# Recurrence scores: four level planes multiplied by masks, four copied over them under masks, two adds for a strided sum

## The reference

```python
def hgrn_chunk(S, q, k, v, logf):
    b = jnp.cumsum(logf, axis=1)
    o_inter = jnp.einsum('bchk,bhkv->bchv', q * jnp.exp(b), S)
    decay = jnp.exp(jnp.where(causal, b[:, :, None] - b[:, None, :], -jnp.inf))
    scores = jnp.sum(q[:, :, None] * k[:, None, :] * decay, axis=-1)
    o_intra = jnp.einsum('btsh,bshv->bthv', scores, v)
    k_dec = k * jnp.exp(b_last[:, None] - b)
    S_new = jnp.exp(b_last)[..., None] * S + jnp.einsum('bchk,bchv->bhkv', k_dec, v)
```

## Time and profile before

| | us |
|---|---|
| median of 3 runs | 1724.35 (1719.77 to 1724.97) |
| the profiled execution | 1728.1 |
| its span | 1726.3 |
| TensorE busy, of the span | 1547.2 (90%) |
| VectorE busy, of the span | 707.1 (41%) |
| ScalarE busy, of the span | 461.9 (27%) |
| L784, 36 of them | 41.5 |
| L786, 36 of them | 64.6 |

### The profile page before, as it was taken

The page is one execution under the profiler, slowest core; times in us unless marked ns, Lnnn a source line. Parts: engine busy times, 40 slices in busy tenths (PEclk is TensorE's granted clock), DMA queues, the critical chain, the costliest instruction groups (busy, mean ns, idle before and its releaser), DMA issues. The chain is left out here.

```text
span 1726.3 us, 22053 instructions
## 1 busy us (share of the span) xinstructions
PE 1547.2 (90%) x7497; PEld 1056.2 (61%) x7498; DVE 707.1 (41%) x1465; ACT 461.9 (27%) x1040; POOL 235.8 (14%) x417
## 2 busy tenths in 40 slices
PE   5999999986899898989789999999799929999996
PEld 3566565665465565655568888888678724444442
DVE  4368886886244453444432222233332241222121
ACT  2233343332233343334332222122232200111110
POOL 1000111011222222222100000000000001122221
PEclk8999999987799998989889999999999959999998
DMA  7001200000402001000055667233343392987973
GB/s 243 26 0 59 78 1 26 1 27 1 143 1 63 1 30 35 1 27 1 27 168 183 199 198 251 80 110 110 132 118 110 110 316 76 336 240 227 302 206 49
DMA packets 119369, 186.03 MB, mean 108 GB/s; under 512 B 9507, under 2 KB 82262, under 8 KB 117222
## 3 DMA queue, kind: packets, MB, share of 16 engines
q1 hardware_dynamic: 107750, 134.41, 24.4%
q0 software_dynamic: 11520, 50.34, 10.0%
HBM read 154.38 MB, written 30.34 MB: 107 GB/s over the span
## 5 line engine op out<-in xcount | busy, mean ns | idle before, releaser
L972 PE MATMUL psum<-attention_part,kept 128*128 128x384 f32 (+1 forms) x576 | 205.6, 513 | 0.7 <-DVE attention_part L1205 0.7
L2166 PE MATMUL psum<-moe_part,kept 128*128 x384 | 172.3, 602 | 6.4 <-issue 4.9
L972 PEld LDWEIGHTS psum<-attention_part,kept 128*128 128x128 f32 (+1 forms) x576 | 110.2, 196 | 78.7 <-issue 20.9
L1438 PE MATMUL psum<-split 128*128 128x368 f32 x384 | 140.6, 366 | 2.5 <-DVE split L1584 2.5
L498 PE MATMUL psum<-kept,recurrence_part 128*128 128x368 f32 x384 | 124.7, 480 | 10.0 <-PEq L236 5.0
L1427 PE MATMUL psum<-kept,sample_part 128*128 128x368 f32 x384 | 131.8, 487 | 1.3 <-PEq L873 1.3
L1440 PE MATMUL psum<-split 128*128 128x368 f32 x384 | 127.3, 332 | 0.0
L2166 PEld LDWEIGHTS psum<-moe_part,kept 128*128 128x128 f32 x384 | 72.3, 193 | 89.6 <-issue 89.6
L1439 PE MATMUL psum<-split 128*128 128x368 f32 x384 | 127.0, 331 | 0.0
L503 PE MATMUL psum<-recurrence_part,kept 128*128 128x512 f32 (+1 forms) x288 | 125.9, 593 | 0.0
L1593 DVE TENSOR_TENSOR merge_part<-merge_part,psum 128x368 f32<-128x368 f32 x48 | 25.8, 538 | 220.2 <-ACT merge_part L1527 220.2
(11 more groups left out here) (312 smaller groups left out, 2527.3 us busy)
## 6 DMA issues: line engine op xcount, KB each, us to landing
sample_part<-merge_gates POOLq DMA_DIRECT2D x16, 1024.0 KB
merge_part<-cache_kT SPq DMA_DIRECT2D x64, 256.0 KB, 3.4
merge_part<-cache_v SPq DMA_DIRECT2D x64, 256.0 KB, 3.1
moe_part<-w_gate SPq DMA_DIRECT2D x16, 1024.0 KB, 6.2
moe_part<-w_up SPq DMA_DIRECT2D x16, 1024.0 KB, 12.6
moe_part<-w_down SPq DMA_DIRECT2D x16, 1024.0 KB, 14.0
recurrence_part<-w_in SPq DMA_DIRECT2D x8, 1024.0 KB, 9.2
sample_part<-merge_out POOLq DMA_DIRECT2D x16, 512.0 KB, 6.4
```

Source lines behind the costliest of these rows:

```text
L972: mm = pe.matmul(bank_of(("z", h, i))[:ROWS[i], 0:384], K["xT"][:, k, cols(i)], Wb[h % 2][:, k, :], start=(k == 0), stop=(k == KC - 1))
L1438: pe.matmul(bank_of(u, 2 * j + 1), wh[w % 2][:, k, ch], xh[b][:, k, :], start=(k == 0), stop=False)
L2166: mm = pe.matmul(psum[:, 2 + par, :], XT[par][:, k, :], K["GU"][:, bass.ds(KC * b + k, 1), :], start=(k == 0), stop=(k == KC - 1))
```

## The change

The buffer `AM` holds four planes in place of eight. The first four planes are multiplied by their masks into it, which sets to 0 every element whose pair belongs to none of them. The other planes (four, or one in tile 0) are copied over it with a predicated copy, element by element where their mask isn't zero; the mask's floats are read as integers for that. As a pair belongs to one plane at most, nothing that is needed is overwritten. Then two adds bring four planes to two and two to one, the second into `AT`. A drain stands between each two. Two instructions of VectorE (L784, L786) become four (L784, L786, L788, L790 in the changed kernel); the lines behind them move down by four, so L806 becomes L810. Nothing changes on the other engines or in the order of the rest.

```diff
@@ -420,7 +420,7 @@
-        AM, AT, kdT = sb(8 * P), sb(2, P), sb(2, P)
+        AM, AT, kdT = sb(4, P), sb(2, P), sb(2, P)
@@ -774,16 +774,20 @@
                 lev = psum[:, 2 + 2 * (s % 2):4 + 2 * (s % 2), :].rearrange("p a (b c) -> p (a b) c", c=P)
-                am = AM[:r, 0:nl * r].rearrange("p (l c) -> p l c", l=nl)
+                mask = (lmask0 if i == 0 else lmask)[:r, :, :r]
                 dve.wait_ge(leveled, s + 1)
                 if s == 0:
                     dve.wait_ge(c_in, 48)
                 if s >= 2:
                     dve.wait_ge(o_done, s - 1)
                 dve.drain()
-                dve.tensor_tensor(am, lev[:r, 0:nl, :r], (lmask0 if i == 0 else lmask)[:r, :, :r], ALU.mult)
+                dve.tensor_tensor(AM[:r, :, :r], lev[:r, 0:4, :r], mask[:, 0:4, :], ALU.mult)
                 dve.drain()
-                dve.tensor_reduce(AT[:r, s % 2, :r], am.rearrange("p l c -> p c l"), AX_X, ALU.add).then_inc(at_done, 1)
+                dve.copy_predicated(AM[:r, 0:nl - 4, :r], mask[:, 4:nl, :].bitcast(I32), lev[:r, 4:nl, :r])
+                dve.drain()
+                dve.tensor_tensor(AM[:r, 0:2, :r], AM[:r, 0:2, :r], AM[:r, 2:4, :r], ALU.add)
+                dve.drain()
+                dve.tensor_tensor(AT[:r, s % 2, :r], AM[:r, 0, :r], AM[:r, 1, :r], ALU.add).then_inc(at_done, 1)
```

## The result

The changed kernel took 1709.12 us in the median of five runs (1704.79 to 1715.82), beside 1724.35 us (1719.73 to 1726.35) for the kernel before: a ratio of 0.9928 with an interval of 0.9899 to 0.9957, 12 us faster. In a second, longer comparison (12 executions against 35) the ratio was 0.9934 (0.9911 to 0.9957), 11.4 us. The forecast was 9.7 us and 1714.6, with a range from 1709 to 1723: the first median lies at its lower edge. The profiled execution has a span of 1714.0 us against 1726.3.

What follows compares the result with a forecast made beforehand. TensorE was taken to bound the recurrence to 343 us, then a ring of VectorE and TensorE. 2.5 + 5.4 + 1.8 (clock) = 9.7 us, taken from 1724.35, gave 1714.6 us; range 1709 to 1723.

Steps and rivals of the forecast that it cites:

- The bound: Recurrence: TensorE sets the pace to 343 us, VectorE is busier behind; VectorE saves 28 us, most beside other work.
- The price of a tile: Four new VectorE instructions hold a full tile for 2.21 us against 3.08, 0.87 us less.
- rival 1: Copy under a mask takes two passes (1721 us) or the strided reduce's rate (1719 us); chance 0.20.
- rival 3: Copy under a mask far from streaming, so tiles get longer: 7.7 us slower, 1732 us; chance 0.07.
- 95 to 343 us: TensorE is full; only three of its four waits for L687 shrink, by 0.87, 0.87 and 0.74: 2.5 us.
- the wait before step 8: TensorE's fourth wait for L687, 1.34 us before 175.30, was to keep its length.
- 343 to 431 us: Last tiles of the recurrence: five give 0.87 us each, tiles 30 and 34 0.5 each: 5.4 us.
- the wait for the root: VectorE's new state waits for GpSimd's L674; in tiles 25, 28 and 31 this swallows the whole saving.
- The clock: End of recurrence: shorter waits put one group of scores at the high TensorE clock, some 1.8 us.
- The sign that was named: TensorE's mean clock over the last 80 us should be above 0.81.
- the ring: Last nine tiles: L784, L786, L806 on VectorE, L518, L519 on TensorE, next L784; the change shortens one link.

Runs made afterwards that it cites:

- the copy-twice kernel: The changed kernel with the copy under masks made twice, a drain between: 1725.06 us, ratio 1.0006 to the kernel before.
- the filler: The changed kernel with four needless products more in each of steps 30 to 35, before TensorE's wait for the new state: 1712.57 us, ratio 0.9915 to the kernel before.

## Why the prediction was right, and where it wasn't

**The bound.** Right. VectorE was to be spared 28 us; by the time that the tiles hold it, it was spared 25.6 (32 x 0.80; its busy time fell by 31.3, from 707.1 to 675.8), and some 9 arrived. Doubling the copy took just this gain back.

**The price of a tile.** Right within a tenth: 2.28 us against 2.21 forecast. The product came out at 693 ns (0.69 forecast), the adds at 427 and 294. The step that no row showed, the copy under a mask, takes 734 ns; taking the row of the same number of streams for it was right, two passes or the reduce's rate (rival 1) wrong, and so was rival 3. The prediction says that what goes is above all the stride of the reduce. The runs show the number of elements first: with half the planes and the stride kept, 0.58 of the 0.80 us were there already. The Trainium skill's advice on the page "VectorE: DVE Perf Modes", section "Rules for kernel authors", sets the number of operations against the number of semaphores, not against their form as the prediction has it; the trace does not follow it, since four instructions of 512, 512, 256 and 128 elements in a row hold VectorE for 2.28 us and two of 1024, one with a stride, for 3.08. The copy-twice kernel holds it as long with five.

**95 to 343 us.** Forecast: 2.5 us, with the wait before step 8 left as it is. The wait for L687 fell by 2.2 us; the waits before 249 and 342 us vanished, that before 316 shrank from 1.28 to 0.44, and that of step 8 stayed (1.34 to 1.70). From the first L519 to that of step 26 the two kernels took 249.3 us (in both traces) and 245.7 and 245.5, so 3.7 us were gained here. A wait of 0.7 us for ScalarE's L584, in both traces before and in neither after, accounts for part of what the sum had left out.

**343 to 431 us.** The wait of L518 fell to 17.4, not to 16 as forecast. From step 26's L519 to the last L556 it was 81.9 and 82.3 us before and 75.8 and 77.7 after: 5.3 us in the mean, with a scatter of 1.9, where 5.4 were forecast without the clock. That the savings of the tiles 25, 28 and 31 end in the wait for the root fits VectorE's waits for it (19.3 us over 95 to 440 us, 9.6 before); that these tiles give their share once ScalarE's order is changed is not shown, as the clock moved as well. Forecast without the clock, the recurrence was to lose 7.9 us; the pairs of traces give 9.7 and 8.4.

**The clock.** This term, 1.8 us, is the step that failed: the runs show nothing in its place. I read from the earlier trace rows that a wait of 2 us or less leaves the clock high, and counted 1.8 us for one group that would be high. In the first trace of the changed kernel the last group ran at the low level (3.23 us) behind a wait of 1.99 us, and in the second trace all four were low. The L518 groups of the steps 30, 33, 34 and 35 add up to 11.67 and 12.27 us in the two traces before, and to 10.87 and 12.75 in the two of the changed kernel: no difference. One trace with few groups at each level does not give a rule: with ScalarE's order changed, groups behind waits of 2.94 and 3.24 us were at the high level. The sign that was named, a mean clock above 0.81, came (0.83), but says nothing: the kernel before had 0.86 in its second trace. The clock is worth 6 us there, as the filler showed, but the change does not collect them. Without this term the forecast is 7.9 us and lies 1.1 us under the mean of the two pairs (9.0); with it, it is 0.7 above.

**The size in all.** The sum came out near for a reason that is partly luck: the clock's 1.8 us, which did not come, made up for 1.2 us before step 26 that were not counted. The timed gains were 15.2 us between the first medians and 11.4 us with more executions (interval 7.4 to 15.3). The second agrees with the recurrence's 9, and its median, 1714.22 us, with the forecast of 1714.6; the first median was 5.5 us under the forecast, within what the attention stage scatters by (14 us over the twelve traces). That nothing behind the recurrence gained is shown by two pairs of traces to no better than this scatter.

## What to carry to other kernels

A sum over planes with a stride is paid for by every element, and laying the data out otherwise only moves the stride to the writer: have fewer elements instead (here masks that exclude each other let one plane be copied over another), and fold what is left by adds of contiguous halves. Before you count a saving on an engine, follow the ring it stands in: here the ring took in about 9 of 26 us, and one split wait on the other engine of the ring gave nearly as much as the change. When such an edit shortens waits, look at the clock of the matmuls behind them before the gain is put down to the wait alone: here filling the waits with needless matmuls gave 5.8 us. Where executions scatter by more than the effect, compare the stage between two instructions of the trace, and take more than one trace of each kernel.

## What was not expected of the hardware

A product that writes 1024 elements 8 apart takes 2019 ns, 793 ns more than in a row, about what the reduce pays for reading 128 apart (693 ns): the write is as sensitive as the read. And matmuls whose results nobody needs, put into waits of some 2 to 4 us, made the scores behind these waits, all but step 32's, run in 1.83 us where they mostly took about 3, and shortened the stage by 6 us.
